# One modulation vector moved out of the three-branch attention into the feed-forward behind it, where VectorE accumulates it

## The chip, the cores and the metric

The kernel runs on one core of a Trainium2 chip. The metric is the device time of one execution in microseconds. Engines are named as in the profile: PE is TensorE, DVE VectorE, ACT ScalarE, POOL GpSimd, SP SyncE, whose instruction queue starts the transfers of weights. "Clock" is the granted clock of TensorE as a share of its full 2.4 GHz; its other level is 1.2 GHz, 0.5 in the rows.

## The reference, cut to what matters

Two blocks of a transformer run over 256 tokens of width 1024 (512 with the context in part of the second). Every sub-layer is modulated by vectors that come from a condition:

```
mod = (silu(c) @ ada_w[layer] + ada_b[layer])          # 9 vectors of 1024 a layer
h = rms_norm(x, g_pre) * (1 + scale) + shift
y = sub_layer(h)                                       # feed-forward, convolution, attention ...
x = x + weight * gate * rms_norm(y, g_post)
# second block, for the tokens and for the context:
mod, modc = silu(c_2) @ ada_w_2 + ada_b_2, silu(c_ctx_2) @ ada_w_2 + ada_b_2
```

Each vector is a product of one row (the condition) with a 1024 x 1024 slice of weights, 4 MB in HBM. The order of the sub-layers is: feed-forward, convolution, feed-forward, shared keys and values, feed-forward, three-branch attention (nsa), feed-forward, differential attention, feed-forward, grouped attention, feed-forward. The change concerns the sixth and the seventh, which stand from 829 to 1003 us and from 1003 to 1205 us in the profile.

## The kernel before, in words

**Weights.** All large products are made in three matmuls from a high and a low part of both operands. A weight unit is 1 MB: SyncE loads it into one of three slots (`stage`, L555), ScalarE rounds it to the high part (`w_hi`, L787), VectorE subtracts to get the low part (`w_lo`, L1217), and TensorE multiplies. A load waits until the low part of the unit three before it is made (`lo_done`). An up step of a feed-forward is two units, one of the gate and one of the up half, each in two groups of columns q; behind it stand ScalarE's silu (L1163) and VectorE's multiply (L1743). A 256-token feed-forward has eleven such steps: three, then a hardware loop of twice three (its body is one code for both passes, i = 1 and 2), then two; the down projection has eleven units more.

**Modulation vectors.** They are made ahead of their use, in a fixed order (`VECS`), each from four loads of 1 MB, its quarters, through a ring of two slots (`ada`, L573). There are two ways to make one:
- on TensorE (`vec_acc`, L1870): a half is two quarters, sixteen matmul rows in the trace, for both conditions at once. VectorE copies the row (L1230), four small matmuls sum it (`vec_sum`, L1881), and VectorE adds the bias (L1243). Inside the attention a half stands at certain values of the loop variable J, by the table `nsa_vec`; its 24 jobs (4 head groups, 2 token tiles, 3 branches) pass through a pipeline of 31 steps J of scores (L2163), softmax on VectorE and ScalarE, transposes (L2180) and the product with the values (L2197).
- on VectorE (`acc_ops`, L1262 and L1264): eight pieces kk, two for each quarter, of the form acc = acc + weights * condition, 128 x 1024 elements. It gives one condition for each stream. TensorE then sums over the partitions with eight matmuls for a stream (`acc_sum`, L1891, sixteen matmul rows in the trace), and VectorE adds the bias (`acc_col`, L1278). This way is taken where `dv` is set; the first feed-forward steps carry four pieces behind step 0 and four behind step 1.

**What is in order.** The order on each engine is that of the code. In SyncE's queue of the feed-forward's first pass stand: unit 3, units 4 and 5, quarters 2 and 3 of the first vector, then, in the loop, units 6 and 7, quarters 0 and 1 of the next vector, units 8 to 11, quarters 2 and 3. A quarter waits until the pieces of the quarter two before it are done (`ring_free`, counted in `acc_s`):

```
            if m != CMP_AT and v in made_by_dve(m + 1):
                return acc_s, 8 * len(made_by_dve(m)) + 2 * (n % VEC_UNITS) + 2
```

and the sum waits for all eight pieces; it stands in the loop's body behind the first unit:

```
                            elif s["dv"] and j == 0 and i is not None:
                                also = {(0, 1): (lambda: acc_sum(s["v"], 5, i),)}
```

## Time and profile before

| | |
|---|---|
| time, 3 runs | 2224.28 us median (2222.31 to 2228.41) |
| profiled execution, its own time | 2224.26 us |
| its span | 2222.2 us |
| mean clock | 0.969 |
| busy: TensorE, VectorE, ScalarE, GpSimd | 95%, 62%, 42%, 4% |
| HBM over the span | 184 GB/s |

A share of busy time is a mean over all stages; the stages differ, so the rows below are taken stage by stage. In a timeline row the first number is the start and the second the duration; the bracket says how long the engine was idle ahead of it and what ended that.

### The profile page before, as it was taken

The numbers are of one execution on the slowest core, as the hardware profiler recorded it, in microseconds if no ns is written. First come the engines' busy times: TensorE is split into PE (matmuls) and PEld (weight loads), VectorE is DVE, ScalarE is ACT, GpSimd is POOL, SyncE is SP. The second block draws the span as 40 slices with busy tenths as digits, with TensorE's granted clock in tenths as the row PEclk, the third lists the DMA queues.
The fourth block names the chain that finished last, engine by engine and source line by source line (L and its number), as shares of the span: only waits on it lengthen the run. The fifth ranks groups of instructions, "written<-read, shape, count | busy, mean of one in ns | idle before, by whom it ended". The sixth has DMA issues, their size and how long they took to land.

```text
span 2222.2 us, 34174 instructions
## 1 busy us (share of the span) xinstructions
PE 2108.4 (95%) x13784; PEld 1869.6 (84%) x13784; DVE 1384.6 (62%) x2044; ACT 934.0 (42%) x1397; POOL 82.6 (4%) x134
## 2 busy tenths in 40 slices
PE   5999999999899999989999999989999999999999
PEld 3998888998899987668987997678888787977997
DVE  2767888677867675547765754956545334856454
ACT  4334434344533454335354544843222223554343
POOL 2000000000100000100000000000000000000000
PEclk9999999999999999979999999999999999999999
DMA  9887675887678847646854221023444232315553
GB/s 326 271 297 270 225 284 199 295 290 257 203 271 278 303 161 253 227 164 210 275 180 161 95 96 58 1 95 120 161 135 151 76 105 76 114 50 197 179 182 114
DMA packets 246620, 411.42 MB, mean 185 GB/s; under 512 B 10237, under 2 KB 191958, under 8 KB 246486
## 3 DMA queue, kind: packets, MB, share of 16 engines
q1 hardware_dynamic: 245840, 409.30, 53.8%
q8 instruction: 95, 1.56, 0.3%
q10 hardware_dynamic: 646, 0.24, 0.0%
q14 instruction: 39, 0.32, 0.0%
HBM read 408.47 MB, written 1.05 MB: 184 GB/s over the span
## 4 chain that ended last, share of the span: by engine, by line
PE 81%; DVE 8%; ACT 4%; DMA 4%; issue 2%; SPq 1%; POOL 1%; ACTq 0%; DVEq 0%
PE bank L1990 20%; PE bank L1939 14%; PE bank L1940 14%; PE bank L1941 14%; PE bank L2063 3%; PE bank L2065 3%; PE bank L2064 3%; PE bank L1891 2%; PE bank L1870 2%; DVE w_lo L1217 1%; DMA ada<-in_ada_w 1%; PE bank L2197 1%; ACT w_hi L787 1%; DVE gate_b L1264 1%; PE bank L1959 1%
## 5 line engine op out<-in xcount | busy, mean ns | idle before, releaser
L1217 DVE TENSOR_TENSOR w_lo<-stage,w_hi 128x2048 fp32r<-128x2048 f32 x255 | 584.2, 2293 | 443.1 <-ACT w_hi L787 442.4
L787 ACT CAST w_hi<-stage 128x2048 fp32r<-128x2048 f32 x255 | 485.4, 1905 | 649.0 <-PE bank L1941 231.6
L1939 PE MATMUL bank<-h_hi,w_hi 128*128 128x256 f32 (+1 forms) x2360 | 710.6, 301 | 2.6 <-ACT mid L960 2.6
L1940 PE MATMUL bank<-h_lo,w_hi 128*128 128x256 f32 (+1 forms) x2360 | 705.8, 299 | 0.0
L1941 PE MATMUL bank<-h_hi,w_lo 128*128 128x256 f32 (+1 forms) x2360 | 705.7, 299 | 0.0
L1939 PEld LDWEIGHTS bank<-h_hi,w_hi 128*128 128x128 f32 x2360 | 452.7, 192 | 19.1 <-issue 5.6
L1940 PEld LDWEIGHTS bank<-h_lo,w_hi 128*128 128x128 f32 x2360 | 452.5, 192 | 15.2 <-issue 1.9
L1941 PEld LDWEIGHTS bank<-h_hi,w_lo 128*128 128x128 f32 x2360 | 452.6, 192 | 13.7
L1990 PE MATMUL bank<-w_hi,h_hi 128*128 128x512 f32 x776 | 247.4, 396 | 13.5 <-DVE h_lo L1226 10.7
L1990 PE MATMUL bank<-w_lo,h_hi 128*128 128x512 f32 x776 | 245.4, 394 | 0.0
L1990 PE MATMUL bank<-w_hi,h_lo 128*128 128x512 f32 x776 | 245.0, 393 | 0.0
L1264 DVE SCALAR_TENSOR_TENSOR gate_b<-ada,cond,gate_b 128x1024 f32<-128x1024 f32 x182 | 231.8, 1283 | 5.6
L1990 PEld LDWEIGHTS bank<-w_hi,h_hi 128*128 128x128 f32 x776 | 146.3, 191 | 46.7 <-issue 12.7
L1990 PEld LDWEIGHTS bank<-w_hi,h_lo 128*128 128x128 f32 x776 | 147.6, 190 | 31.4
L1990 PEld LDWEIGHTS bank<-w_lo,h_hi 128*128 128x128 f32 x776 | 147.6, 190 | 31.3
L2063 PE MATMUL bank<-w_hi,h_hi 128*128 128x256 f32 (+1 forms) x552 | 159.0, 288 | 7.3 <-issue 4.3
L2064 PE MATMUL bank<-w_lo,h_hi 128*128 128x256 f32 (+1 forms) x552 | 157.2, 285 | 0.0
L2065 PE MATMUL bank<-w_hi,h_lo 128*128 128x256 f32 (+1 forms) x552 | 157.1, 285 | 0.0
L1743 DVE TENSOR_TENSOR mid<-silu_t,bank 128x256 f32 (+3 forms) x132 | 61.1, 463 | 149.2 <-PE bank L1941 149.2
L1163 ACT ACTIVATE silu_t<-bank 128x256 f32<-128x256 f32 (+1 forms) x132 | 54.5, 417 | 214.4 <-PE bank L1941 205.6
L2063 PEld LDWEIGHTS bank<-w_hi,h_hi 128*128 128x128 f32 x552 | 107.3, 194 | 8.7 <-issue 6.4
L2064 PEld LDWEIGHTS bank<-w_lo,h_hi 128*128 128x128 f32 x552 | 107.3, 194 | 0.0
(251 smaller groups left out, 2026.0 us busy)
## 6 DMA issues: line engine op xcount, KB each, us to landing
ada<-in_ada_w SPq DMA_DIRECT2D x114, 1024.0 KB, 5.4
stage<-in_ffn_w_in SPq DMA_DIRECT2D x88, 1024.0 KB, 8.5
stage<-in_ffn_w_out SPq DMA_DIRECT2D x44, 1024.0 KB, 5.1
stage<-in_ffn_w_gu SPq DMA_DIRECT2D x44, 1024.0 KB, 5.1
stage<-in_ffn_w_down SPq DMA_DIRECT2D x22, 1024.0 KB, 4.9
stage<-in_a_w_in SPq DMA_DIRECT2D x12, 1024.0 KB, 7.8
stage<-in_diff_w_in SPq DMA_DIRECT2D x12, 1024.0 KB, 5.1
ada<-in_kv_ada_w SPq DMA_DIRECT2D x8, 1024.0 KB, 5.7
```

The costliest lines, as they stand in the source:

```text
L787: a.copy(w_hi[:, s, :], stage[:, s, :]).then_inc(hi_done, 1)
L1163: a.activation(silu_t[:, q, 0:T], bank[q][:, 0:T], ACT.Silu).then_inc(silu_done, 1)
L1217: v.tensor_tensor(w_lo[:, s, :], stage[:, s, :], w_hi[:, s, :].bitcast(F32), ALU.subtract).then_inc(lo_done, 1)
L1264: ins = v.scalar_tensor_tensor(out=acc[c], in0=w, scalar=cond[:, b, kk, c:c + 1], in1=acc[c], op0=ALU.mult, op1=ALU.add)
L1743: v.tensor_tensor(mid[:, bass.ds(o, T)], silu_t[:, q, 0:T], bank[2 + q][:, 0:T], ALU.mult).then_inc(mid_done, 1)
L1939: m.matmul(dst[:, 0:T], wh, h_hi[:, h0:h0 + T], start=(k == ks[0]), stop=False)
L1940: m.matmul(dst[:, 0:T], wh, h_lo[:, h0:h0 + T], start=False, stop=False)
L1941: ins = m.matmul(dst[:, 0:T], wl, h_hi[:, h0:h0 + T], start=False, stop=(k == ks[-1]))
L1990: ins = m.matmul(y_bank(T, tt, h)[:, :], a_[:, r:r + P], w_[:, slot, kc * D + h * 512:kc * D + (h + 1) * 512], start=first and n == 0, sto ...
L2063: m.matmul(dst, h_hi[:, r], w_hi[:, slot, c], start=(k == ks[0]), stop=False)
L2064: m.matmul(dst, h_hi[:, r], w_lo[:, slot, c], start=False, stop=False)
L2065: ins = m.matmul(dst, h_lo[:, r], w_hi[:, slot, c], start=False, stop=(k == ks[-1]))
```

## The change

The attention makes five vectors in place of six, at ten places J instead of twelve. The feed-forward behind it makes four in place of three. The first of these four feeds the second block's feed-forward, which has tokens and context, and is made for both conditions: two streams. Its pieces are spread over three steps. The fourth vector takes the places that the five-vector feed-forwards have for theirs.

```diff
-        add("nsa", io["b_w_in"][0], io["b_w_out"][0], 256, 6, 14, norm_col(1, 1, 0), norm_col(1, 1, 1), one, 5, 1, 4)
-        add("ffn", io["ffn_w_in"][1, 1], io["ffn_w_out"][1, 1], 256, 3, 17, norm_col(1, 2, 0), norm_col(1, 2, 1), half, 11, 2, 11)
+        add("nsa", io["b_w_in"][0], io["b_w_out"][0], 256, 5, 14, norm_col(1, 1, 0), norm_col(1, 1, 1), one, 5, 1, 4)
+        add("ffn", io["ffn_w_in"][1, 1], io["ffn_w_out"][1, 1], 256, 4, 17, norm_col(1, 2, 0), norm_col(1, 2, 1), half, 11, 2, 11)
...
-        nsa_vec = {2 + 2 * n: (n // 2, n % 2) for n in range(12)}
+        nsa_vec = {2 + n * 11 // 5: (n // 2, n % 2) for n in range(10)}
...
-            return 2 if subs[8]["v"] <= vi < subs[8]["v"] + subs[8]["nvec"] else 1
+            return 2 if vi == subs[6]["v"] or subs[8]["v"] <= vi < subs[8]["v"] + subs[8]["nvec"] else 1
+
+        def streams_of(vi, i):
+
+            return 1 if vi == subs[6]["v"] and i is not None else streams(vi)
...
-                    if s["nvec"] == 5 and j == 1:
+                    if s["nvec"] >= 4 and s["dv"] and j == 1:
                         load_vec(s["v"] + 3, *ada_src(s["v"] + 3), 1)
...
-                        if s["nvec"] == 5 and k == 9:
+                        if s["nvec"] >= 4 and s["dv"] and k == 9:
                             load_vec(s["v"] + 3, *ada_src(s["v"] + 3), 0)
...
-                    for c in range(streams(vi)):
+                    for c in range(streams_of(vi, i)):
                         if kk == 0:
                             ins = v.tensor_scalar(acc[c], w, cond[:, b, kk, c:c + 1], None, ALU.mult)
                         else:
...
-                                if j < 2:
+                                if i is None and streams(s["v"]) > streams(s["v"] + 1):
+                                    acc_ops(s["v"], range(3 * j, min(3 * j + 3, KC)))
+                                elif j < 2:
                                     acc_ops(s["v"], range(4 * j, 4 * j + 4), i)
...
-                        if s["nvec"] == 5:
+                        if s["nvec"] >= 4:
                             acc_ops(s["v"] + 3, range(0, 4) if j == 9 else range(4, 6))
...
-                    if s["nvec"] == 5:
+                    if s["nvec"] >= 4 and s["dv"]:
                         if j < 2:
                             acc_ops(s["v"] + 3, (6 + j,))
                         if j == 3:
                             acc_col(s["v"] + 3, 2)
-                        if j in last_acc:
+                        if j in last_acc and s["nvec"] == 5:
                             acc_ops(s["v"] + 4, last_acc[j])
...
-                        if j == 2 and s["nvec"] == 5:
+                        if j == 2 and s["nvec"] >= 4:
                             pe.wait_ge(mid_done, s["c"] + 2 * nb)
                             acc_sum(s["v"] + 3, 2)
```

VectorE in the first three steps of the feed-forward, where `w_lo` is the low part of a unit, `mid<-silu_t,bank` the multiply of a step and `gate_b<-ada` a piece of the vector. Before:

```order
L1217 TENSOR_TENSOR w_lo<-stage,w_hi 128x2048 x3
L1743 TENSOR_TENSOR mid<-silu_t,bank 128x256 x2
L1262 TENSOR_SCALAR gate_b<-ada,cond 128x1024
L1264 SCALAR_TENSOR_TENSOR gate_b<-ada,cond,gate_b 128x1024 x3
L1217 TENSOR_TENSOR w_lo<-stage,w_hi 128x2048 x2
L1743 TENSOR_TENSOR mid<-silu_t,bank 128x256 x2
L1264 SCALAR_TENSOR_TENSOR gate_b<-ada,cond,gate_b 128x1024 x4
L1217 TENSOR_TENSOR w_lo<-stage,w_hi 128x2048 x2
L1743 TENSOR_TENSOR mid<-silu_t,bank 128x256 x2
```

The same place of the changed kernel:

```order
L1221 TENSOR_TENSOR w_lo<-stage,w_hi 128x2048 x3
L1747 TENSOR_TENSOR mid<-silu_t,bank 128x256 x2
L1266 TENSOR_SCALAR gate_b<-ada,cond 128x1024 x2
L1268 SCALAR_TENSOR_TENSOR gate_b<-ada,cond,gate_b 128x1024 x4
L1221 TENSOR_TENSOR w_lo<-stage,w_hi 128x2048 x2
L1747 TENSOR_TENSOR mid<-silu_t,bank 128x256 x2
L1268 SCALAR_TENSOR_TENSOR gate_b<-ada,cond,gate_b 128x1024 x6
L1221 TENSOR_TENSOR w_lo<-stage,w_hi 128x2048 x2
L1747 TENSOR_TENSOR mid<-silu_t,bank 128x256 x2
L1268 SCALAR_TENSOR_TENSOR gate_b<-ada,cond,gate_b 128x1024 x4
```

Eight operations came in, and piece 3, the last of the first four, moved from behind step 0 to behind step 1, past two `w_lo` and the multiplies; pieces 6 and 7 moved behind step 2.

TensorE inside the attention around the steps J = 21 to 24, with the scores `bank<-mid`, the transposes `bank<-ident`, the halves of a vector `bank<-ada,cond` and their sums `bank<-sel,ada_row`. Before:

```order
L1870 MATMUL bank<-ada,cond 32x512 x8
L2180 MATMUL bank<-ident,gate_b 15x128 x4
L2197 MATMUL bank<-mid 128x64 x4
L2163 MATMUL bank<-mid 128x15 x4
L2180 MATMUL bank<-ident,gate_b 128x128 x8
L2197 MATMUL bank<-mid 128x64 x4
L2206 MATMUL bank<-ident,mid 128x128 x2
L1870 MATMUL bank<-ada,cond 32x512 x8
L2180 MATMUL bank<-ident,diag 128x128 x8
L2197 MATMUL bank<-mid 128x64 x8
L2180 MATMUL bank<-ident,silu_t 15x128 x4
L1881 MATMUL bank<-sel,ada_row 128x4 x4
```

The same stretch of the changed kernel, up to the last steps, which hold no vector:

```order
L1876 MATMUL bank<-ada,cond 32x512 x8
L2186 MATMUL bank<-ident,silu_t 128x128 x4
L2203 MATMUL bank<-mid 128x64 x4
L2169 MATMUL bank<-mid 128x256 x4
L2186 MATMUL bank<-ident,gate_b 15x128 x4
L1887 MATMUL bank<-sel,ada_row 128x4 x4
L2203 MATMUL bank<-mid 128x64 x4
L2169 MATMUL bank<-mid 128x15 x4
L2186 MATMUL bank<-ident,gate_b 128x128 x8
L2203 MATMUL bank<-mid 128x64 x4
L2212 MATMUL bank<-ident,mid 128x128 x2
L2186 MATMUL bank<-ident,diag 128x128 x8
```

The last half stood at J = 24, in front of the transposes of that step; it is now at J = 21, with its sum a step behind it.

## Rows read from the trace of the kernel before

**Rows 1.** The page: busy time, and the chain that ended last by engine.

```profile
PE 2108.4 (95%) x13784; PEld 1869.6 (84%) x13784; DVE 1384.6 (62%) x2044; ACT 934.0 (42%) x1397; POOL 82.6 (4%) x134
...
PE 81%; DVE 8%; ACT 4%; DMA 4%; issue 2%; SPq 1%; POOL 1%; ACTq 0%; DVEq 0%
```

**Rows 2.** Busy time by stretches: length, engines, clock, DMA share, GB/s.

```profile
856.00:972.00 116.00, 107.25 (x818) 74.23 (x816) 59.68 (x335) 48.23 (x165) 11.64 (x16) 0.87 0.60 211
1016.00:1053.00 37.00, 37.00 (x311) 37.00 (x311) 26.34 (x22) 15.15 (x15) 0.00 (x0) 1.00 0.89 297
```

**Rows 3.** Groups of instructions, 856 to 972: busy, mean ns, idle ahead.

```profile
L1870 PE MATMUL bank<-ada,cond 128*32 128x512 f32 x192 | 29.2, 716 | 6.0 <-DMA ada<-in_ada_w 6.0
...
L1881 PE MATMUL bank<-sel,ada_row 128*128 128x4 f32 x48 | 5.8, 244 | 0.3 <-DVE mid L1520 0.3
```

**Rows 4.** TensorE's timeline, J = 10 and 12; stretches behind J = 12, at J = 24.

```profile
890.89 1.92 PE L1870 MATMUL bank<-ada,cond 128*32 128x512 f32 x16
...
900.78 1.06 PE L1870 MATMUL bank<-ada,cond 128*32 128x512 f32 x8 [1.98 <-DMA ada<-in_ada_w]
...
901.80:908.00 6.20, 6.20 (x48) 5.97 (x44) 2.74 (x13) 0.68 (x2) 0.00 (x0) 0.72 0.71 260
...
953.00:957.50 4.50, 3.82 (x17) 0.42 (x17) 1.37 (x5) 0.00 (x0) 0.70 (x1) 0.50 1.03 374
```

**Rows 5.** Timeline: two streams in the later feed-forward; sums of one and two.

```profile
1525.91 1.41 DVE L1262 TENSOR_SCALAR gate_b<-ada,cond 128x1024 f32<-128x1024 f32 x2
1527.36 7.58 DVE L1264 SCALAR_TENSOR_TENSOR gate_b<-ada,cond,gate_b 128x1024 f32<-128x1024 f32 x6
...
1052.43 1.84 PE L1891 MATMUL bank<-ones,gate_b 128*128 128x4 f32 x16
...
1579.44 3.63 PE L1891 MATMUL bank<-ones,gate_b 128*128 128x4 f32 x32
```

**Rows 6.** VectorE's timeline in the feed-forward's first pass.

```profile
1025.02 3.99 DVE L1264 SCALAR_TENSOR_TENSOR gate_b<-ada,cond,gate_b 128x1024 f32<-128x1024 f32 x3
...
1035.76 5.31 DVE L1264 SCALAR_TENSOR_TENSOR gate_b<-ada,cond,gate_b 128x1024 f32<-128x1024 f32 x4
...
1046.94 0.42 DVE L1743 TENSOR_TENSOR mid<-silu_t,bank 128x256 f32<-128x256 f32 x1 [0.99 <-PE bank L1941]
...
1060.28 0.42 DVE L1743 TENSOR_TENSOR mid<-silu_t,bank 128x256 f32 x1 [2.19 <-PE bank L1941]
```

**Rows 7.** SyncE's issues; landing of those at 1029.76 and 1041.87; spread 845 to 1000.

```profile
1029.04 0.37 SPq L573 DMA_DIRECT2D ada<-in_ada_w  x1
...
1029.76 0.38 SPq L555 DMA_DIRECT2D stage<-in_ffn_w_in  x1
...
stage<-in_ffn_w_in SPq DMA_DIRECT2D x1, 1024.0 KB, 7.6
...
1041.87 0.37 SPq L555 DMA_DIRECT2D stage<-in_ffn_w_in  x1
...
stage<-in_ffn_w_in SPq DMA_DIRECT2D x1, 1024.0 KB, 8.6
...
DMA to landing us min/median/max: 4.9/6.4/9.3
```

**Rows 8.** The page: the low and high part of a unit.

```profile
L1217 DVE TENSOR_TENSOR w_lo<-stage,w_hi 128x2048 fp32r<-128x2048 f32 x255 | 584.2, 2293 | 443.1 <-ACT w_hi L787 442.4
L787 ACT CAST w_hi<-stage 128x2048 fp32r<-128x2048 f32 x255 | 485.4, 1905 | 649.0 <-PE bank L1941 231.6
```

**Rows 9.** TensorE after the boundary; stretches there and at the attention's end.

```profile
1007.32 1.70 PE L1950 MATMUL bank<-ident,mid 128*128 128x128 f32 x8 [4.00 <-DVE mid L1346]
...
1009.00:1014.00 5.00, 3.88 (x19) 3.90 (x19) 2.89 (x9) 3.48 (x6) 2.99 (x5) 0.50 0.00 0
...
953.00:977.00 24.00, 20.39 (x91) 14.70 (x92) 10.06 (x26) 5.47 (x7) 2.14 (x3) 0.57 0.23 78
```

**Rows 10.** TensorE's timeline: transposes for the next stage, in the down projection.

```profile
1159.72 1.09 PE L1950 MATMUL bank<-ident,mid 128*128 128x128 f32 x8 [1.47 <-DVE mid L1346]
```

More of the change, by code:

```diff
@@ L221, in add @@
                      b=N["bstep"], sc=N["silu"], sb=list(N["step"]), g_pre=g_pre, g_post=g_post, weight=weight,
-                     post=g_post is not None, late=4 if nvec == 5 else 1 if kind == "conv" else None, units=steps * parts, bsteps=bsteps)
+                     post=g_post is not None, late=4 if nvec == 5 and kind == "ffn" else 1 if kind == "conv" else None, units=steps * parts, bsteps=bsteps)
             N["unit"] += steps * parts + bsteps
@@ L280, in has_vec @@
         def has_vec(s, i):
-            return s["dv"] or s["nvec"] == 3 or s["nvec"] == 1 and i is None
+            return s["dv"] or s["nvec"] == 1 and i is None
         def pause_bank(nxt):
@@ L627, in one_unit @@
                         load_vec(s["v"] + 1, *ada_src(s["v"] + 1), 1)
-                    if s["nvec"] == 5 and j == 1:
+                    if s["nvec"] >= 4 and s["dv"] and j == 1:
                         load_vec(s["v"] + 3, *ada_src(s["v"] + 3), 1)
-                    if s["nvec"] == 5 and j in (6, 10):
+                    if s["nvec"] == 5 and s["dv"] and j in (6, 10):
                         load_vec(s["v"] + 4, *ada_src(s["v"] + 4), j // 10)
```

## The prediction

> **What bounds the kernel now.** I read the page first: busy shares and the chain that ended last. TensorE is busy for 95% of the span and holds 81% of the chain [rows 1]. A microsecond counts only if it is TensorE's own work or a time in which TensorE waits. Then the table by stretches [rows 2]. In the three-branch attention (856 to 972 us) TensorE is busy for 107 of 116 us and VectorE for 60. In the first pass of the feed-forward behind it (1016 to 1053) TensorE never stops and VectorE is busy for 26.3 of 37 us. Next the groups of instructions inside the attention: the matmuls that multiply a vector's weights by the condition (L1870) hold 29.2 us and 6.0 us of waiting for their transfers, 35.2 us for twelve halves, and the sums behind them (L1881) 5.8 us for six [rows 3]. Last the timeline: a half that finds its data takes 1.92 us, one that doesn't takes over 4, with part of it and of the work behind it at a granted clock of about 0.5, the 1.2 GHz level [rows 4].
>
> **What goes out of the attention.** One vector: two halves of 1.92 us and a sum of about 0.8 us (the 5.8 us of group 3 over six are 0.97 with the overlap of the last result): 4.6 us. VectorE's two operations of it lie in its idle half.
>
> The ten halves left stand at J = 2, 4, 6, 8, 10, 13, 15, 17, 19, 21 instead of 2, 4, ..., 24. Twelve halves at 1.92 us are 23.0 us; the other 12.2 of the 35.2 are waiting and half clock. A load goes out when its slot is released, so the spacing counts. 116 us less 35.2 and 5.8 leave 75 us for 31 steps, 2.4 us each: two steps and a half are 6.8 us, while the second load of a half lands some 8 us after the half began. Two places can be read. The half at J = 12 waited 1.98 us for its second load, and the 6.2 us behind it had a mean clock of 0.72, which costs 0.28 x 6.2 = 1.7 us; it has now three steps of room, so these 3.7 us go. The half at J = 24 fills the stretch from 953.0 to 957.5, 3.8 of 4.5 us busy at a clock of 0.50, 2.6 us over a clean one, and its wait and slow clock go out with it [rows 4]. Against these 6.3 us the halves at 15, 17 and 21 now fall into other steps, some of them short; I charge 1.6 us, my choice. Sum: 4.6 + 4.7 = **9.3 us less**. Bounds: 4.6 if every wait comes back elsewhere, 4.6 + 12.2 = 16.8 if none is left.
>
> **What comes into the feed-forward, first pass.** Call its weight units u0, u1, ...; one step of TensorE is two units and takes 11.5 us. The first vector now needs both conditions. Two streams are in the trace in the later feed-forward: 1.41 us for the opening pair and 7.58 for six operations, so 2.52 us for a piece of two, against 3.99 for three pieces of one stream [rows 5, 6]. Eight extra operations at 1.26 and 0.7 are 9.5 us on VectorE, which has 10.7 us idle in that pass; by totals they fit. The order decides otherwise. Pieces 0 to 2 stand behind step 0, 3 to 5 behind step 1, 6 and 7 behind step 2. The load of quarter 3 waits until piece 3 is done, and on SyncE's in-order queue the load of u6 stands behind it. Before, piece 3 closed step 0: quarter 3 went out at 1029.04, u6 at 1029.76 [rows 6, 7]. Now:
> - pieces 0 to 2 from 1024.2: 1.41 + 4 x 1.26 = 6.4, to 1030.7; two w_lo operations of 2.29 to 1035.3; multiplies, bound to TensorE, to 1036.0; piece 3 to 1038.5.
> - quarter 3 goes out at 1038.7, u6 at 1039.4, 9.6 us later than before. u6 took 7.6 us to land with quarter 3 ahead of it [rows 7]: 1047.0. ScalarE 1.9, VectorE 2.3 [rows 8]: ready at 1051.3. TensorE wants it at 1046.9 (the multiply that it released then, rows 6). **Pause of 4.4 us.** By the same steps from 1029.76 it could be ready at 1041.6 before, 5.3 us ahead; 9.6 less 5.3 is the pause again.
> - u7: ScalarE's two silus and its w_hi to 1051.5, VectorE to 1053.8, multiplies to 1054.6, pieces 6 and 7 (four operations, 5.05) to 1059.7. TensorE is through u6 at 1057.1 to 1059 and then waits for them, since the first sum needs all pieces. It starts that sum at 1059.8, before at 1052.4: **7.4 us late**, the pause included.
> - the sum has two streams: 3.48 us by the 32-matmul row against 1.74 by the 16-matmul row (starts to the next instruction) [rows 5]: 9.1 late. u7 ends at 1069.0.
> - the next vector's quarter 1 waits for piece 7, with u8 behind it: out at 1060.5 (was 1041.87), landed 7.6 later, ready at 1072.4. **Pause of 3.4 us.** Before, TensorE was through u7 at 1060.2 [rows 6]: 12.2 late.
> - behind a pause TensorE restarts at half clock: after 4.00 us of idleness at the boundary the clock was still 0.50 from 1009 to 1014 [rows 9]. Some 3 us of it behind the second pause cost 1.4 us. The same loss in u6 lies under its wait. **13.6 late.**
> From there VectorE has room again (8 operations of one stream in 38 us) and the queue catches up: u12 would go out at 1079.5 and be wanted at 1096.
>
> **The rest of it.** The loop's body is one code for both passes, so the second sum has two streams as well: 1.7 us. The fourth vector's own sum in the down projection: 1.7 us. Its eight operations stand in steps 9, 10 and the first units of the down projection. One of them and the two ahead push VectorE there, and the transposes for the next stage already waited 1.47 us for VectorE [rows 10]: I take 0.6 us (0 if the idle time in front of its w_lo absorbs them, 1.3 if one operation shows in full). SyncE's four added loads go out behind pieces that are long done; the pool engine is untouched; the two added small modv operations are under 0.2 us each. Sum: 13.6 + 1.7 + 1.7 + 0.6 = **17.6 us more**. Bounds: with the shortest landing of this stretch's kind, 4.9 us, both pauses lose 2.7, with no half clock and no 0.6: 10.2. With 8.6 us, the landing that u8 had, 1 us more at each pause, a half-clock loss of 2.8 and 1.3 at the end: 21.7. I take 7.6 because u6 had it with the same load ahead.
>
> By the Trainium skill (DMA: Bandwidth & Descriptors, "Anatomy of one DMA — SWDGE (gpsimd) path") a transfer costs 2.0 us and its bytes at 436 GB/s; it gives this for the gpsimd path. An estimate by this page is 4.4 us for 1 MB, each pause would be 3.2 us shorter, and the sum would be 11.2 instead of 17.6. The trace doesn't agree: the load of 1 MB with another ahead took 7.6 [rows 7]; the rival "covered" below is what the page would make of it.
>
> On the clock the rows differ: a pause of 1.98 us was followed by a mean of 0.72 over 6.2 us [rows 4], one of 4.00 by 0.50 that lasted longer [rows 9]. The Trainium skill (TensorE: Matmul & The Clock Gate, "HAM oscillation — how this bites in real kernels") says that waits for transfers can return the array to its slow state each time; by that each of the two pauses costs more than its length, without it the 1.4 us fall away.
>
> **Sum.** 2222.2 us of span, 2224.26 us of the profiled execution, which is the median of the runs shown (2224.28) within 0.02. 2224.26 + 17.6 - 9.3 = **2232.6 us**.
>
> **The rivals.**
> - *Covered (0.28).* u6 and u8 land in about 5 us as transfers with nothing ahead do, and the clock stays up: 10 to 12 us in, 9.3 out, 2226. For it: the shortest landing is 4.9. Against: both stand right behind another 1 MB.
> - *The attention at full pace (0.10, faster).* With fewer loads none of the halves waits and TensorE keeps the 2.4 GHz level to the end: 16.8 us go, and of the tail, 24 us at a mean clock of 0.57 [rows 9], some 4 more, 21 in all. It decides once the feed-forward costs under 14 us: with its lower bound, 2224.3 - 21 + 10.2 = 2213.5. For it: the waits are there. Against: a two-step gap is still 6.8 us against 8.
> - *The block repeats (0.10, slower).* The lateness of VectorE and the queue isn't caught up in the second pass and one more pause of 4 us with its clock follows, near 2238.
> - *It doesn't do what I read.* Another order on SyncE than I read, so that u6 isn't held: the sums (5.2) and the pieces in front of the first one (2.6) are in, 9.3 are out: 2223, 0.02.
>
> **How the numbers follow.** The forecast has 0.50, with a range of its own of 2228 to 2239. A measurement of this kernel tells 0.3%, 6.7 us, from no change: slower is above 2231.0, faster below 2217.6. Slower: three quarters of the forecast's own range and half of that beside it lie above, 0.44, with the repeating block 0.54. Faster: 0.10. Between them 0.36. The range of 2224 to 2239.5 leaves out the faster case and the ends.
>
> **What would show it.** In the trace after: the attention some 106 to 108 us long instead of 116; TensorE idle for 3 to 6 us before the seventh weight unit of the feed-forward, SyncE's load of it right behind a modulation load and 9 to 10 us later than before; then a short wait for gate_b before 32 matmuls of the sum; another pause two units on; granted clock near 0.5 behind them; no pause in the second pass. I am wrong if TensorE stays busy there (the queue isn't the block), or if the attention shrinks by over 13 us.

## The result, and the profile after

The changed kernel takes 2253.64 us (median of four, 2244.44 to 2254.22), the kernel before 2223.3 us beside it: a ratio of 1.0119, 95% interval 1.0093 to 1.0146. It is slower by 30 us. I had forecast 2232.6 us and a range up to 2239.5. The side was right, the size was not.

The page of the changed kernel, busy time and the chain by engine, to be held against [rows 1]:

```profile
PE 2120.0 (95%) x13792; PEld 1882.2 (84%) x13792; DVE 1402.4 (63%) x2060; ACT 933.3 (42%) x1397; POOL 83.1 (4%) x134
...
PE 78%; DVE 10%; DMA 4%; ACT 4%; issue 2%; POOL 1%; SPq 0%; ACTq 0%; DVEq 0%
```

TensorE runs eight rows more and is busy 11.6 us longer: each microsecond of its work counts, but so does the speed at which it works.

**The feed-forward.** TensorE's longest waits from 1004 to 1130 us (total, times, longest):

```profile
PE bank L1945 <- DVE w_lo L1221: 4.7, 2, 4.2
PE bank L1956 <- DVE mid L1350: 4.0, 1, 4.0
PE bank L1897 <- DVE gate_b L1268: 2.1, 1, 2.1
```

The wait of 4.0 is the old one at the boundary [rows 9]. The two others are new and stand where the prediction put them: one for the low part of u6, one for pieces 6 and 7 in front of the first sum. SyncE's issues in the same pass, against [rows 7]:

```profile
1024.77 10.44 SPq L577 DMA_DIRECT2D ada<-in_ada_w  x2
1035.56 1.11 SPq L559 DMA_DIRECT2D stage<-in_ffn_w_in  x2
1040.09 17.58 SPq L577 DMA_DIRECT2D ada<-in_ada_w  x2
1058.27 12.62 SPq L559 DMA_DIRECT2D stage<-in_ffn_w_in  x4
```

Quarters 2 and 3 went out at 1024.77 and some 10 us later. Only then, at 1035.56, came u6, 36.7 us behind the boundary (the first transposes of this feed-forward, at 998.90). Before it was 27.5 us (1029.76 less 1002.22), so it is 9.1 us later, where 9.6 were forecast; with nothing in its way (e3 below) it went out 26.2 us behind the boundary. VectorE shows the same from its side, against [rows 6]:

```profile
1032.34 7.58 DVE L1268 SCALAR_TENSOR_TENSOR gate_b<-ada,cond,gate_b 128x1024 f32<-128x1024 f32 x6
1045.22 2.29 DVE L1221 TENSOR_TENSOR w_lo<-stage,w_hi 128x2048 fp32r<-128x2048 f32 x1 [5.31 <-ACT w_hi L791]
...
1052.13 4.99 DVE L1268 SCALAR_TENSOR_TENSOR gate_b<-ada,cond,gate_b 128x1024 f32<-128x1024 f32 x4
1068.07 2.29 DVE L1221 TENSOR_TENSOR w_lo<-stage,w_hi 128x2048 fp32r<-128x2048 f32 x1 [10.95 <-ACT w_hi L791]
```

VectorE, which got eight operations more here, stands idle for 5.31 and 10.95 us in front of the low parts of u6 and u8: their data isn't there. TensorE's timeline at u6, at the first sum and at the second:

```profile
1047.65 0.38 PE L1945 MATMUL bank<-h_hi,w_hi 128*128 128x256 f32 x1 [4.25 <-DVE w_lo L1221]
...
1057.25 5.66 PE L1897 MATMUL bank<-ones,gate_b 128*128 128x4 f32 x32 [2.10 <-DVE gate_b L1268]
...
1099.38 3.63 PE L1897 MATMUL bank<-ones,gate_b 128*128 128x4 f32 x32
```

Two stretches of the same kernel, behind the first sum and around the second (length, TensorE busy, clock, DMA share, GB/s):

```profile
1058.00:1066.00 8.00, 8.00 (x44) 0.57 0.96 321
...
1099.00:1107.00 8.00, 8.00 (x59) 0.79 0.82 259
```

The sum of two streams took 5.66 us at half clock behind the pauses, and 3.63 in the second pass.

**The attention.** Its stretch shrank by only 3.3 us in this profile, and in others of the same kernel it was longer than before. So I took three profiles of each unchanged kernel (e8 and e14 are the kernel before, e1 and e15 the changed one). Each stretch has fixed ends, read from TensorE's timeline: the attention from the first to the last products on bank<-mid (scores and values), the feed-forward from the transposes that open it (the boundary, 1002.22 and 998.90) to those that open the differential attention, and the rest to the end of the span. The rows of the kernel before (columns as in [rows 2]: length, busy time of the engines, clock, DMA share, GB/s):

```profile
854.08:968.74 114.66, 107.45 (x827) 75.21 (x828) 59.88 (x339) 48.23 (x165) 10.92 (x15) 0.87 0.63 220
1002.22:1210.41 208.19, 200.79 (x1405) 187.97 (x1405) 139.02 (x150) 96.34 (x120) 8.37 (x11) 0.98 0.66 220
1210.41:2222.20 1011.79, 969.06 (x5744) 836.49 (x5744) 561.23 (x805) 411.83 (x644) 25.05 (x33) 0.98 0.33 110
```

The changed kernel:

```profile
853.95:965.57 111.62, 102.22 (x787) 73.62 (x788) 59.55 (x336) 47.79 (x165) 10.92 (x15) 0.88 0.54 189
998.90:1225.84 226.94, 213.20 (x1452) 199.71 (x1452) 157.22 (x169) 96.22 (x120) 8.88 (x11) 0.95 0.65 220
1225.84:2242.60 1016.76, 973.53 (x5744) 838.91 (x5744) 561.31 (x805) 411.46 (x644) 25.04 (x33) 0.97 0.33 110
```

The table has the same stretches of all kernels that ran. "At full clock" is the length times the mean clock of its row; the remainder is lost to half clock. The rows give the clock to two digits, so these figures are good to 0.6 us in the attention and to 1 us in the feed-forward. "Softmax" is TensorE's waiting for VectorE's and ScalarE's copies in front of transposes and products of the attention (L1520, L1524, L1562, L1019 and their like).

| kernel | attention | clock | at full clock | waits: transfers, softmax | feed-forward | rest |
|---|---|---|---|---|---|---|
| before | 114.7 | 0.87 | 99.8 | 6.0, 1.1 | 208.2 | 1011.8 |
| before, e8 | 109.4 | 0.92 | 100.7 | 6.0, 1.0 | 207.6 | 1012.5 |
| before, e14 | 110.0 | 0.93 | 102.3 | 7.5, 1.1 | 208.2 | 1013.0 |
| changed | 111.6 | 0.88 | 98.2 | 3.8, 5.2 | 226.9 | 1016.8 |
| changed, e1 | 116.5 | 0.84 | 97.8 | 4.1, 5.0 | 228.4 | 1014.5 |
| changed, e15 | 117.1 | 0.84 | 98.4 | 4.1, 5.0 | 227.3 | 1017.1 |
| e2 one stream | 116.7 | 0.82 | 95.7 | 3.2, 5.0 | 210.1 | 1016.4 |
| e3 single swap | 116.3 | 0.84 | 97.7 | 4.2, 5.0 | 226.2 | 1017.2 |
| e4 late places | 112.0 | 0.87 | 97.4 | 2.6, 5.6 | 226.8 | 1017.0 |
| e5 units first | 122.6 | 0.79 | 96.9 | 3.7, 5.1 | 221.1 | 1012.5 |
| e6 small loads | 109.6 | 0.86 | 94.2 | 0, 5.6 | 227.9 | 1017.2 |
| e7 short halves | 115.4 | 0.84 | 96.9 | 3.8, 5.3 | 226.9 | 1016.9 |
| e9 dummy halves | 111.2 | 0.92 | 102.3 | 5.0, 0.8 | 228.1 | 1016.7 |
| e10 filler | 112.4 | 0.95 | 106.8 | 1.2, 1.7 | 224.5 | 1012.8 |
| e11 filler, before | 117.3 | 0.94 | 110.3 | 3.3, 0.8 | 208.4 | 1012.8 |
| e12 units, one sum | 116.9 | 0.84 | 98.2 | 3.9, 5.0 | 215.1 | 1017.3 |
| e13 three edits | 109.5 | 0.95 | 104.0 | 6.2, 0.8 | 218.8 | 1014.4 |

Means of the three unchanged pairs: attention 111.4 and 115.1, feed-forward 208.0 and 227.5, rest 1012.4 and 1016.1. These are +3.7, +19.5 and +3.7, together 26.9, and the spans (2219.7 and 2246.8) differ by 27.1. The medians above differ by 30.3; the first profile of the changed kernel fell on the shortest of its four executions (2244.44 us, the others 2253.40 to 2254.22), so the profiles show some 3 us less than the medians.

The waits for the softmax that are new in the attention have fixed places. The two longest aren't at its end. TensorE's timeline of the changed kernel at J = 12 and J = 18 (counted by the groups of scores, L2169):

```profile
900.78 0.66 PE L2186 MATMUL bank<-ident,diag 128*128 128x128 f32 x4 [1.52 <-DVE mid L1562]
...
927.28 0.66 PE L2186 MATMUL bank<-ident,gate_b 128*128 128x128 f32 x4 [1.52 <-DVE mid L1562]
```

And the stretch behind J = 18 (length, TensorE busy, clock, DMA share, GB/s):

```profile
929.00:935.50 6.50, 6.50 (x36) 0.50 0.00 1
```

Both steps held a half before and lost it by the new table of places (13 and 17, 19 in their stead). e1 and e15 have the same two waits of 1.52 us. The other new ones, 0.6 to 0.9 us each, stand in the steps J = 23 and 24, behind the last half. So of some 4.5 us of new waiting 3.0 stand in steps that the choice of the ten places left empty.

### The profile page after: what moved, and what is told of

It is laid out like the page before. It is cut to its first block, busy times and chain, and to the rows that moved or that the text cites. A ratio compares the mean times of both kernels' runs of the same rounds, so it can differ in the third digit from the quotient of the medians.

```text
span 2242.6 us, 34212 instructions
## 1 busy us (share of the span) xinstructions
PE 2120.0 (95%) x13792; PEld 1882.2 (84%) x13792; DVE 1402.4 (63%) x2060; ACT 933.3 (42%) x1397; POOL 83.1 (4%) x134
## 4 chain that ended last, share of the span: by engine, by line
PE 78%; DVE 10%; DMA 4%; ACT 4%; issue 2%; POOL 1%; SPq 0%; ACTq 0%; DVEq 0%
PE bank L1996 20%; PE bank L1945 13%; PE bank L1946 13%; PE bank L1947 13%; PE bank L2069 3%; PE bank L2071 3%; PE bank L2070 3%; DVE w_lo L1221 2%; DMA ada<-in_ada_w 2%; DVE gate_b L1268 2%; PE bank L1897 2%; PE bank L1876 1%; ACT w_hi L791 1%; PE bank L2203 1%; DMA stage<-in_ffn_w_in 1%
## 5 line engine op out<-in xcount | busy, mean ns | idle before, releaser
L1996 PE MATMUL bank<-w_hi,h_hi 128*128 128x512 f32 x776 | 247.3, 396 | 13.6 <-DVE h_lo L1230 10.8
L1268 DVE SCALAR_TENSOR_TENSOR gate_b<-ada,cond,gate_b 128x1024 f32<-128x1024 f32 x196 | 249.2, 1283 | 5.7
```

The source lines that it names most:

```text
L1268: ins = v.scalar_tensor_tensor(out=acc[c], in0=w, scalar=cond[:, b, kk, c:c + 1], in1=acc[c], op0=ALU.mult, op1=ALU.add)
L1996: ins = m.matmul(y_bank(T, tt, h)[:, :], a_[:, r:r + P], w_[:, slot, kc * D + h * 512:kc * D + (h + 1) * 512], start=first and n == 0, sto ...
```

## The experiments

**e1, the changed kernel again.**

> The changed kernel once more, nothing edited. Its profiled execution took 2244.4 us at a mean clock of 0.964, the three others 2253 to 2254 at 0.958 to 0.959. If those are two settings of one kernel (theory A: the same work, but some half-clock stretches more, so 0.006 x 2250 = 13 us lost to the clock), this run's profile or its timed executions show times of both kinds or of the slow kind, with the extra time spread over stretches of lower granted clock and no new wait. If the short one was an outlier (theory B), all executions take 2252 to 2255 and the profile shows where the other 10 us are.

Measured: 2250.04 us (2247.53 to 2253.94), ratio to before 1.0129, 1.0093 to 1.0165. Its profile has a span of 2245.8 us at a clock of 0.961. Times in between the two kinds, so it is a spread, and theory A in this form (two settings) is too simple. What A said of the cause holds: against the first profile the attention lost 5 us more to the clock at the same work (97.8 against 98.2 at full clock).

**e2, one stream.** Left out: the context's condition of the first vector, which gets a copy of the other (the lines for the copy aren't shown).

```diff
-            return 2 if vi == subs[6]["v"] or subs[8]["v"] <= vi < subs[8]["v"] + subs[8]["nvec"] else 1
+            return 2 if subs[8]["v"] <= vi < subs[8]["v"] + subs[8]["nvec"] else 1
```

> The first vector of the feed-forward for one condition only (what is left out: its context condition, which gets a copy of the other); pieces again four behind step 0 and four behind step 1, sums of 16 matmuls. Theory A (the second stream and the queue block behind it cost the time in the first pass): the feed-forward has its old pace there, no pause at its seventh and ninth weight unit, 13.6 + 1.7 us less, 17 in all with the slower clock, so 2235 to 2239 against 2253. Theory B (the loss comes with the fourth vector or out of the attention): under 5 us less, 2248 or more.

Measured: 2234.29 us, ratio 1.0053, 1.0025 to 1.0081. Theory A: the feed-forward takes 210.1 us against 227.5, 17.4 less, with no wait for a low part. What is left of its cost, 2.1 us, comes with the fourth vector. But the kernel is still 7 us slower than before, though one vector went out of the attention: its attention took 116.7 us.

**e3, the single swap on SyncE.** Its order of loads around unit 6:

```diff
...
+                        unit(5)
+                        quarter(2)
+                        unit(6)
+                        quarter(3)
...
```

> Only SyncE's order changes in this feed-forward: the load of the seventh weight unit goes ahead of quarter 3 of the vector made then, and the ninth ahead of quarter 1 of the next one (in all passes). All arithmetic stays. Theory A (the units are late because they stand in the queue behind a quarter that waits for a piece): both pauses of TensorE go, with their half clock, 4.4 + 3.4 + 1.4 = 9 us less; the wait of the first sum for pieces 6 and 7 stays at 3 us or so; 2244 against 2253. Theory B (VectorE itself is behind with the low parts, 9.5 us of added operations): the units land earlier but their low parts are ready no earlier, under 3 us less.

Measured: 2250.01 us, ratio 1.0130, 1.0094 to 1.0166, no gain. By the time alone theory B would have won. SyncE's rows say otherwise:

```profile
1030.55 0.47 SPq L559 DMA_DIRECT2D stage<-in_ffn_w_in  x1
1040.20 0.37 SPq L577 DMA_DIRECT2D ada<-in_ada_w  x1
1040.92 0.38 SPq L559 DMA_DIRECT2D stage<-in_ffn_w_in  x1
...
1058.64 0.38 SPq L577 DMA_DIRECT2D ada<-in_ada_w  x1
1059.29 4.89 SPq L559 DMA_DIRECT2D stage<-in_ffn_w_in  x3
```

u6 goes out at 1030.55 instead of behind quarter 3, but u7 now stands behind it (1040.92) and u9 behind quarter 1 of the next vector (1059.29). The pause for w_lo is gone, the wait for gate_b grew from 2.1 to 3.8 us. The block was handed on by one unit.

**e5, units first.** The same edit with the order unit 6, unit 7, quarter 3, unit 8, quarter 0, units 9 and 10, quarter 1, unit 11.

> As the run before with another order on SyncE, but so that in the first pass no weight unit stands behind a quarter whose piece isn't done yet: units 6 and 7 ahead of quarter 3, then unit 8, quarter 0, units 9 and 10, quarter 1, unit 11. In that run the single swap only handed the block on (unit 7 went out at 1040.9 behind quarter 3, unit 9 at 1059.3 behind quarter 1). Theory A (the queue block costs the pauses): no pause before a low part in the whole stage, first sum 46 us behind the boundary (53 in the changed kernel, 49 with the single swap), second 83 to 86 behind it (95, 93), stage 9 to 12 us shorter, 2239 to 2242. Theory B (VectorE's added 9.5 us are the loss, in whatever place): the second sum stays over 90 us behind the boundary.

Measured: 2243.31 us, ratio 1.0090, 1.0059 to 1.0121. The waits of its feed-forward:

```profile
PE bank L1985 <- DVE mid L1379: 6.3, 3, 4.0
PE bank L1958 <- ACT h_hi L898: 0.9, 1, 0.9
PE bank L1926 <- DVE gate_b L1297: 0.8, 1, 0.8
PE bank L1974 <- DVE w_lo L1250: 0.4, 1, 0.4
```

Of 4.7 and 2.1 us of waiting, 0.4 and 0.8 are left. The stage takes 221.1 us, 6.4 less than the mean of the changed kernel and not the 9 to 12 I expected; the second sum came 92.8 us behind the boundary (1103.15 less 1010.40), in the changed kernel 100.5. My figures of 46 and 83 to 86 were counted from the second group of transposes, 5.1 us later: from there the first sum came after 46.0 us, as expected, and the second after 87.7. The queue block is real: 6.4 us by the stage, 7.7 at the second sum. By the kernel's time alone e5 isn't told from the changed kernel: the intervals overlap (1.0059 to 1.0121, 1.0093 to 1.0146). The same profile has the longest attention of all, 122.6 us at a clock of 0.79, for code that wasn't touched.

**e12, units first and the second condition's sum once.** The second stream's accumulator isn't overwritten by the later vectors, so its sum can wait for step 9:

```diff
...
-                for st in range(streams(vi)):
+                for st in (0, 1) if vi == v6 + 2 else (0,) if vi == v6 else range(streams(vi)):
...
```

> The kernel with the weight units ahead of the quarters, 2243.3 us, and the second condition's sum made once, with the third vector's at step 9, where it stood in the body of the loop and so in both passes. Theory A (each pass pays 1.7 us for it, and the clock falls behind the long run of small matmuls in the second pass): 1.7 us less by the sums alone, up to 1.7 more by the clock, 2239 to 2242. Theory B (the sums are covered by waits for VectorE anyway): 2243 or more.

Measured: 2238.72 us, ratio 1.0058, 1.0038 to 1.0078, on theory A's side, though this interval and e5's overlap. The feed-forward takes 215.1 us, 6.0 less than e5's, and 1.4 of this at full clock (221.1 x 0.96 = 212.2 against 215.1 x 0.98 = 210.8), which agrees with the 1.7 of the sums as far as clocks of two digits can tell. The other 4.6 are half clock that didn't come; how much of that is the edit's is open, since e13 below took 218.8 us for the same stage.

**e4, halves up to J = 24.**

```diff
-        nsa_vec = {2 + n * 11 // 5: (n // 2, n % 2) for n in range(10)}
+        nsa_vec = {2 + n * 22 // 9: (n // 2, n % 2) for n in range(10)}
```

> Only the ten places in the attention change: J = 2, 4, 6, 9, 11, 14, 16, 19, 21, 24, so that the last half stands again where it stood before. Theory A (the attention gained 3.3 us where 9.3 were forecast because its tail, without a half in it, waits for the softmax on VectorE and ScalarE at half clock): halves spread to the tail fill these waits, and the boundary behind the attention comes 2 to 5 us earlier. Theory B (the halves' own waits for transfers are what is left, wherever they stand): within 1.5 us of the changed kernel.

Measured: 2246.62 us, ratio 1.0109, 1.0072 to 1.0147. Attention 112.0 us, inside the spread of the changed kernel, with as much waiting for the softmax (5.6). Inconclusive by its length. The waits tell more: the half is back at J = 24, but the steps J = 12 and 18 still hold none, and each still waits 1.52 us (1.63 at J = 23). So the missing half at the end isn't the whole of it.

**e6, small loads.** Left out: seven eighths of these vectors' weights.

```diff
+                    if subs[5]["v"] <= v < subs[5]["v"] + subs[5]["nvec"]:
+                        a, dst = a[:, :, 0:128], dst[:, :, 0:128]
```

> The loads of the five vectors in the attention bring 128 of each 1024 columns (left out: seven eighths of these weights, the rest of the slot keeps older ones); all instructions stay. From the first scores to the boundary: 145 to 150 us in four executions with ten halves, 148 with twelve. Theory A (halves wait for their transfers and the array falls to half clock behind the waits; two halves fewer at wider places bought nothing because these waits stayed): the stretch falls by 6 to 10 us, its mean clock rises from 0.85 towards 0.95. Theory B (the steps of the pipeline wait for VectorE and ScalarE, and the halves lie in these waits): within 2 us.

Measured: 2246.23 us, ratio 1.0115, 1.0078 to 1.0152. No wait for a transfer is left. The attention takes 109.6 us, 5.5 less than the changed kernel's mean, and at full clock it falls to 94.2, 3.9 under the mean of 98.1, as much as the waits for transfers (4.0) that went. The clock stays at 0.86, and the waits for the softmax are still there (5.6 us). Theory A holds for the waits and fails for the clock.

**e7, short halves.** Left out: three quarters of these products.

> Each half in the attention multiplies a quarter of its weights: 4 matmul rows of 16 (left out: three quarters of the product); loads and semaphores stay. This takes 10 x 1.44 = 14 us of TensorE's own work out of the stretch. Theory A (TensorE's work there is on the path, as my sum had it): 10 to 14 us shorter. Theory B (the steps are bound by the loads' pace and by the softmax, the halves' matmuls fill waits): under 5 us shorter, and TensorE's idle time in the stretch grows by the rest.

Measured: 2254.94 us, ratio 1.0146, 1.0115 to 1.0177. This run tells nothing on its question, since its premise was wrong; its attention (115.4 us) is that of the changed kernel. A half of 4 matmul rows took as long as one of 16. From the timeline of e7:

```profile
883.21 1.90 PE L1877 MATMUL bank<-ada,cond 128*32 128x512 f32 x4
```

1.90 us here, 1.92 for sixteen rows [rows 4]. The rows left out worked in other 32-column groups of the array, beside the ones that stayed. The Trainium skill (TensorEngine Tiling (Array Packing), "Key Properties") says that different tiles can execute in parallel; the two rows agree.

**e8, the kernel before again.**

> The kernel before once more, nothing edited, for a second profile. One profile gave 148.1 us from the first scores to the boundary, and 1011.8 us from the first transposes of the differential attention to the end. Theory A (removing the sixth vector gained nothing in the mean, the 3.3 us of one pair of profiles was scatter): a stretch of 146 to 149 again. Theory B (it gained 3 or more): 150 to 153. Behind the differential attention's start the changed kernels took 1014 to 1017: if that is scatter of the clock, this run gives 1013 to 1017 too.

Measured: 2222.44 us (ten runs), ratio 0.9999. Its attention is 109.4 us, from the first scores to the transposes behind the down projection 142.8, shorter than in the first profile and than the 146 to 149 of theory A. So removing the vector gained nothing in the mean: theory A, and more than it said. Behind the differential attention's start it took 1012.5 us, not the 1013 to 1017 that would have made the longer rest of the changed kernels scatter.

**e9, dummy halves.** Two halves on data that is there already, at J = 22 and 24; the ten real ones at 2, 4, ..., 20.

```diff
-        nsa_vec = {2 + n * 11 // 5: (n // 2, n % 2) for n in range(10)}
+        nsa_vec = {2 + 2 * n: (n // 2, n % 2) for n in range(10)}
...
+                    elif J in (22, 24):
+                        if J == 22:
+                            pe.wait_ge(ada_rowed, rowed(rv(s["v"] + 4)))
+                        for k in range(8):
+                            for h in range(2):
+                                z = 32 * (2 * (k % 2) + h)
+                                m.matmul(bank[7][z:z + 32, :], cond[:, 0, k, :], xs[:, 0, h * 512:(h + 1) * 512], start=True, stop=True, tile_position=(0, z))
```

> The changed kernel with its ten halves at J = 2, 4, ..., 20 and, at J = 22 and 24, two dummy halves: 16 matmul rows each on the condition and the residual, results unused, no loads. So TensorE's work of the twelve halves is back, the four loads and one sum are not. From the first to the last scores the stretch took 114.7 and 109.4 us with twelve halves (14.7 and 8.6 of it lost to half clock, 100.0 and 100.8 at full clock) and 111.6 to 122.6, mean 116.7, with ten (lost 13.1 to 25.5, 95.9 to 98.5 at full clock). Theory A (the halves' work keeps the clock up; taking it out is paid back in half clock): lost 8 to 15, stretch 109 to 114, the kernel 3 to 5 us faster than the changed one, 2246 to 2249. Theory B (the scatter of the clock has nothing to do with the halves): lost near 19 as with ten, the stretch 119 or more, the kernel 3 us slower.

Measured: 2245.61 us (2240.94 to 2247.18), ratio 1.0090, 1.0070 to 1.0110. In the trace each dummy half has 32 rows and 3.64 us, twice a real half, so I added more work than I had said. The stretch took 111.2 us all the same, 3.9 less than the changed kernel's mean, with 102.3 at full clock and 8.9 lost instead of 17. Theory A, with one thing that I left mixed: the run also puts the real halves back on the even steps, J = 12 and 18 among them, and the two waits of 1.52 us there are gone. What the dummies did and what the places did isn't told apart; the ten real halves at 2, 4, ..., 20 alone weren't run. In the tail, the last steps, the dummies do it. A wait in TensorE's timeline of the changed kernel (e15):

```profile
958.68 0.66 PE L2186 MATMUL bank<-ident,gate_b 128*128 128x128 f32 x4 [0.73 <-ACT mid L1019]
```

The stretch around it, in the columns of the stretches above:

```profile
957.00:974.00 17.00, 15.04 (x78) 13.60 (x76) 5.81 (x25) 7.72 (x16) 2.18 (x3) 0.58 0.00 0
```

The same place in e9, TensorE's timeline:

```profile
955.51 3.64 PE L2183 MATMUL bank<-xs,cond 128*32 128x512 f32 x32
959.08 1.09 PE L2193 MATMUL bank<-ident,diag 128*128 128x128 f32 x8
```

And e9's stretch around it:

```profile
949.00:966.00 17.00, 16.22 (x146) 10.93 (x138) 6.21 (x28) 7.50 (x18) 2.19 (x3) 1.00 0.00 1
```

With a half in front of them the transposes find their data, and the clock stays at 1.00 over 17 us. Without it TensorE stops in front of them, and works the same stretch at 0.58.

**e10, filler in each step without a half.** Four matmuls of 32 x 512 (eight rows in the trace) ahead of the wait for the exponentials.

```diff
...
+                        for z in range(0, 128 if J not in nsa_vec else 0, 32):
+                            m.matmul(bank[4 + nsa_slot["t", i, 0] % 2][z:z + 32, :], cond[:, 0, 0, :], xs[:, 0, 0:512],
+                                     start=True, stop=True, tile_position=(0, z))
...
```

> The changed kernel with four matmuls of 32 x 512 (one for each group of array columns, side by side, 0.47 us at full clock, results unused) in front of the wait for the exponentials in each step of the attention without a half. Theory A (waits let the clock fall): lost under 10 us instead of 13 to 25, for at most 6 us of added work that isn't hidden in waits; stretch 106 to 112 against 116.7. Theory B (clock independent of it): stretch as long as with ten halves or up to 6 us longer, lost near 19.

Measured: 2243.55 us, ratio 1.0089, 1.0068 to 1.0109. The clock rises to 0.95, the loss falls from 17 to 5.6 us, the waits for the softmax from 5.1 to 1.7, and the work at full clock grows by 8.7: 112.4 us in all, 2.7 under the mean of the changed kernel. Here the halves keep their places, so this run shows without e9's mixture that filled waits go with a higher clock. Theory A for the clock; the filler costs most of what it gives. I had taken one at 0.47 us, at most 6 in all. In TensorE's timeline it takes about twice that:

```profile
902.43 1.06 PE L2182 MATMUL bank<-xs,cond 128*32 128x512 f32 x8
```

**e11, the same filler in the kernel before.**

> The same filler in the kernel before (ten steps without a half in J = 2 to 24, one in its tail). Theory A: lost under 8 us instead of 8.6 to 14.7, the kernel within 4 us of before on either side, faster if the waits hide the filler. Theory B: 3 to 6 us slower than before.

Measured: 2230.56 us (twelve executions, one of them an outlier of 4165.68 us), ratio 1.0020, 1.0003 to 1.0038: slower by little. 110.3 us at full clock against 100.9, lost 7.0 against 10.5. Where the steps already hold twelve halves there is little waiting for the softmax to fill (1.1 us before, 0.8 here), and theory B's price is paid.

**e13, three edits: e12 with the dummy halves.**

> Three edits together: weight units ahead of the quarters, the second condition's sum once, and the two dummy halves at J = 22 and 24 in the attention. If the two causes are separate and add (theory A), the feed-forward keeps its 215 us and the attention, from the first to the last scores, falls from 117 to 109 to 113 with 8 to 12 lost to half clock: 2231 to 2236, still 7 to 12 us behind the kernel before. If the slower attention only moves the loss elsewhere (theory B), the sum of both stretches stays and the kernel at 2238 or more.

Measured: 2233.28 us, ratio 1.0044, 1.0028 to 1.0061. The time and the length of the attention (109.5 us, 7.4 less than e12's) are as theory A has them, and with 5.5 us it lost less to the clock than the 8 to 12 expected; the feed-forward lost more to the clock than in e12. Both stretches together are 328.3 us against 332.0, so the two causes add at least in part; the intervals of e12 and e13 overlap, and how fully they add isn't settled. No version beat the kernel before.

**e14 and e15, third profiles of both.**

> A third profile of the kernel before, nothing edited. If twelve halves keep the clock up (theory A): first to last scores 109 to 115 us with 8 to 15 lost; from the first transposes of the differential attention to the end 1006 to 1008 with 22 lost. If those two profiles were luck (theory B): 116 or more, lost 18 or more; behind it 1009 or more.

> A third profile of the changed kernel, nothing edited. Theory A: first to last scores 111 to 123 us with 13 to 25 lost; feed-forward 227 to 228; from the differential attention on 1009 to 1012 with 25 to 29 lost. Theory B: attention under 111, or the rest at 1006 to 1007 as in the kernel before.

Measured: 2221.18 and 2253.85 us, spans 2219.1 and 2252.1. Theory A in the attention: 110.0 us with 0.93, and 117.1 with 0.84. The rest, behind the differential attention's start, took 1013.0 and 1017.1 us, 5 us more than I had expected of either kernel.

## Why the prediction was wrong, step by step

**The queue block: right.** In the profile of the changed kernel the pause before u6 was 4.25 us (4.4 forecast). The first sum came 58.35 us behind the boundary's transposes against 50.21, 8.1 late (7.4 forecast), the second 100.5 against 86.6, 13.9 late (13.6), the third 140.1 against 122.9, 17.2 late (15.3). The stage as a whole grew by 18.7 us in that profile and by 19.5 in the mean, against 17.6. Inside, two terms were off and cancelled: the second pause was 0.5 us and not 3.4, because TensorE, at half clock through the first sum and u7, came late itself. The half clock that I priced at 1.4 us came to over 8: 227.5 us hold 12.9 of it in the mean, 208.0 held 4.2. So the net work and waits of the stage are 10.8 us, and the clock's share is 8.7. Nor did TensorE restart at half clock behind the first pause, as I had written: the first matmuls behind it start every 0.12 us, and only from 1048.6 on, 1 us later, every 0.21. Of the 1.9 us missing at the third sum 1.6 fell in the second pass, where the clock dropped to 0.79 around the second long run of small matmuls, a place at which I had none. It isn't there each time: in e1 it was 0.71 behind that sum, in e15 1.00.

**The attention: wrong. "4.6 + 4.7 = 9.3 us less" was the step that failed.** It was 3.7 us more, 13 us off, and this is most of the error. Three parts of it:
- *"One vector: 4.6 us" of TensorE's own work.* It did go out, but I counted it as if nothing stood behind it. TensorE's waits for the softmax were 1.0 to 1.1 us in all three profiles with twelve halves and 5.0 to 5.2 in all three with ten. Steps that lost their half have nothing in front of their transposes: J = 12 and 18 by the new places (1.52 us each), the last ones because no half is left for them. About 4 us of the work's 4.6 came back as waiting. At J = 12 I had looked at the wait for the load alone: it went, as forecast, and a wait for the softmax took its place.
- *The waits for transfers*, those at J = 12 and J = 24 among them, did shrink, from 6.5 us in the mean to 4.0. Work, softmax and transfers together are 4.6 - 4.0 + 2.5 = 3.1 us; the rows give 2.8 at full clock (100.9 to 98.1), the same within their two digits.
- *The clock.* I took the wait and the half clock behind it as one thing that leaves together. What was lost to half clock rose from 10.5 to 17.0 us. New waits, in other places, go with it: with them filled the loss was 5.6 us in e10 and 8.9 in e9, and with every wait for a transfer gone but these left it was 15.3 in e6. The Trainium skill (TensorE: Matmul & The Clock Gate, "A second HAM failure mode: psum-queue depth-cycling") tells of another kernel in which short idle times between groups of matmuls are enough for the clock to go to and fro; the traces agree: the waits in the tail are 0.6 to 0.9 us long, and the clock there is 0.58 with them (e15) and 1.00 in e9, where only one of 0.61 and one of 0.17 us are left, at its very end.

How much of the 13 us is the number of halves and how much their places stays open. The bounds, 4.6 to 16.8 us less, left out a loss, and with it went the range. The lower bound assumed that removed work is always gained. The tail's own rows would have warned me: its mean clock was 0.57 before, and the half at J = 24 was the last thing that filled it.

**The rest: not foreseen.** From the differential attention on both kernels run the same instructions (x5744), yet the changed one takes 3.7 us more in the mean; in the first pair TensorE is idle equally long (42.7 and 43.2 us in the rows above) and busy 4.5 us longer, so it is clock. Kernels e5, e10 and e13, all with the changed feed-forward, had 1012.5, 1012.8 and 1014.4. So the longer rest doesn't come each time with the change. Whether it goes with the moment at which the stages begin isn't shown; what decides it stays open. I had taken stretches that aren't edited as constant.

**The sum.** 17.6 less 9.3 was 8.3 us. The chip gave 19.5 + 3.7 + 3.7, and 0.2 around them, 27.1 between the spans. The rival that ended higher (the block repeats) didn't come: there is no pause in the second pass. The chance of "slower" was added too high as well: three quarters of a part of the 0.50 and half of the other part are at most 0.375, with the repeating block 0.48 and not 0.54.

## What to carry to other kernels

Work of the bounding engine is not always worth its time: where it stands ahead of a wait, ask what fills the wait when it is gone, and what the idle time does to the clock of what stands behind. Put independent matmuls into the steps that wait, and when some go, look at which steps are left empty. When an in-order queue carries two kinds of loads, and one kind waits for work that gets slower, move all urgent loads ahead of it: moving one only hands the block on. And before a term of a few microseconds is read from one profile, take a second profile of the same kernel; here one stretch varied by over 5 us between profiles of one kernel.

## What the hardware showed that I had not expected

- The same instructions took 95.7 to 98.4 us at full clock and 111.6 to 122.6 us in fact, in seven profiles of an attention with identical code (changed, e1, e15, e2, e3, e5, e12). The clock's loss alone ranged from 13 to 26 us.
- A stretch with two groups of 3.64 us of useless matmuls more, and the real ones on other steps, was shorter (115.1 to 111.2 us): the clock rose from 0.85 to 0.92.
- Four matmul rows of 32 columns' width took 1.90 us where sixteen, in four column groups, took 1.92.
